# Modulation units of the front by feature tile, with the q and k products between them, and the decay product on four column tiles

## The chip, the core and the metric

One core of a Trainium2 chip runs the whole program. The metric is the device time of one launch in microseconds, the median of several executions. Everything is float32; an instruction of the matrix engine that is a product stands in the trace as two MATMULs.

## The reference

Two layers of a hybrid decoder step on 256 prompt tokens and 8 single decode tokens (264 columns in all), with 1024 features. What the change touches is the very start of layer 0:

```
m = silu(c) @ w_ada + b_ada                 # 9 conditioning rows -> 3 x 1024
shift, scale, gate = split(m, 3)
h = x * (1 + scale) + shift
z = h @ w_in                                # 1024 -> q 256, k 256, v 512, g 512, a_lr 16, u 1024
log_a = log_sigmoid(a_lr @ w_a2 + b_a) / 16 # 16 -> 256, the decay of the linear attention
glu = ua * sigmoid(ug)                      # u = [ua, ug]
```

After it come a gated linear attention over 4 heads, a causal convolution of 31 taps over 512 channels of `glu`, an output projection, layer norm, a mixture of 16 experts (each 3 matrices of 2 MB), and a second layer with a pooling mixer and another mixture.

## The kernel before

Features lie on the partitions: x and h are 8 tiles of 128 features by 264 tokens (`x[:, k, :]`, `h[:, k, :]`). Weights come in units of 2 MB, 128 partitions x 8 row tiles x 512 columns, into nine slots (six in `ring`). `load_plan` lists the units with their slots in the order in which SyncE issues them (L492 to L496, `fill`): the four modulation units of layer 0's shift and scale, `ada` 0 to 3 (each 512 columns of `w_ada`, in rows of 2 KB), then the unit of q and k (`qk`), the masks of `con` (L494), `ug`, `ua`, `v`, `g`. SyncE waits for a slot to be free (`unit_free`); the matrix engine waits for a unit by the slot's semaphore (`unit_ready`, with the count in `FILL`). ScalarE's queue loads x_prompt, x_sample and ten small vector tensors (L1092 to L1098). GpSimd's queue loads the 16 columns of the decay's first matrix (`walr`, L1854) and its second (`wa2`, L1856), then waits until all of h is there (`h0_ready` 8) and loads the convolution history, conv_w, the attention state (L1860 to L1866) and the router's matrices of both layers (ten loads of 16 KB, L1868 and L1871). The state lands where x_prompt was.

The order of work on the matrix engine is written out by hand. It transposes silu(c) (L811), runs modulation unit 0 (`ada_unit`: 32 instructions on four column tiles that give 9 rows, L567; ScalarE copies them, `ada_columns` at L586 turns them into columns), transposes the vectors (L817) and x (L825; ScalarE copies each tile, scaled), and runs units 1 to 3. Since unit i holds columns 512i to 512i + 511, units 0 and 1 are all the shifts and 2 and 3 all the scales: no tile of h can be made before unit 3 is through. VectorE then adds the bias (`ada_copy`), makes the samples' part of h in two operations and the eight tiles in eight (`modulate0`, L1403 to L1411), each tile a count of `h0_ready`.

`z_tile` (L831) makes the tiles of the projection in the order of `Z_TILES`: the decay's first product `alr` (L841: 8 products of 16 columns, each on a tile of h), q tile 0 (L850, 8 products), `la` 0 and 1 (L844, the decay's second product, which waits for the copy of `alr`), the other three of q and k, then level 0 of the attention (L868), then for each further level s two more tiles and the level: `ug0` and `ua0` before level 1, and so on. Bank numbers are in `Z_BANK`. VectorE and ScalarE make from `la` the log decay and its two running sums (L1487), on which level 1 rests, while level 0 needs only q and k.

Of the kernel before, what the change touches and what calls it, by code (L numbers as in the profile page):

```python
# [25 lines left out]
P = 128  # L26
# [3 lines left out]
NS = 8  # L30
# [73 lines left out]
FILL = {n: [s for m, s in PLAN[:i + 1] if len(m) == 2].count(SLOT[n]) for i, (n, _) in enumerate(PLAN)}  # L104
# [67 lines left out]
def build(nc, I, O):  # L172
    with ExitStack() as ctx:
# [75 lines left out]
        walr = t2f[:, 1536 + SEQ:1536 + SEQ + KD * 16].rearrange("p (k n) -> p k n", k=KD)  # L249
# [134 lines left out]

        def ada_slice(i):
            s, n = divmod(i, ADA_UNITS)
            return ksplit(I["w_ada"][s // 2, s % 2][:, FF * n:FF * (n + 1)])
# [27 lines left out]
        N_ROWS, N_SMALL, N_ROUTE, N_HIST = len(VEC_ROWS), 2, 14, 2  # L415
# [11 lines left out]
        Z_BANK = [0, 1, 2, 3, 4, 5, 0] + [4 + i % 2 for i in range(16)]  # L427
# [27 lines left out]
        def _(sp):  # L455
# [95 lines left out]
        def _(pe):  # L551
# [22 lines left out]
            def ada_columns():  # L574
# [4 lines left out]
                s, n = divmod(i, ADA_UNITS)  # L579
                taken = [p[:2] for p in PIECES].index((s, n)) if (s, n) in [p[:2] for p in PIECES] else 0  # L580
# [3 lines left out]
                for b in range(2):  # L584
                    o = ada_bank(i)[:, 36 * n:36 * (n + 1)].rearrange("p (h b w) -> p b h w", h=2, b=2)[:, b]
                    last = mm(o, ada_rows[:, i % 2, P * b:P * (b + 1)], fold, start=True, stop=True)  # L586
# [226 lines left out]
            ada_unit(0)  # L813
            pe.wait_ge(s_rows, 16 * N_ROWS)
            for i, n in enumerate((96, 90, 124)):
                o = (0, 96, 186)[i]
                last = tr(bank[4][:, o:o + n], rowsA[0:n, i, :], ident[0:n, 0:n])  # L817
            last.then_inc(E("opening_tr"), 1)
# [8 lines left out]
            for i in range(1, ADA_FRONT):  # L827
                ada_unit(i)
            ada_columns()

            def z_tile(i):  # L831
# [1148 lines left out]
```

## Time and profile before

| | us |
|---|---|
| median of 3 runs (lowest, highest) | 852.32 (851.91, 852.33) |
| profiled execution, in all | 850.87 |
| its span, from the first to the last instruction | 849.0 |
| matrix engine busy | 741.4 (87%) |
| VectorE, ScalarE, GpSimd busy | 240.7, 282.3, 130.0 |
| DMA, mean rate | 330 GB/s |
| mean granted clock of the matrix engine | 0.947 |

The stretch of the change is the first 60 to 70 us. Read the chain for what ends last, the timeline for durations, and the DMA views for what the queues move: q1 is SyncE's queue, q10 ScalarE's, q0 GpSimd's.

### The profile page before, as it was taken

Reading aid. Unit: us, or ns where it says so; the run is one execution under the profiler, and the core shown is the slowest. Engines: PE = TensorE matmul, PEld = TensorE weight load, DVE = VectorE, ACT = ScalarE, POOL = GpSimd, SP = SyncE. Lnnn points to the kernel's source line nnn. Section 1 sums busy time; section 2 is a strip of 40 time slices with the busy share of each in tenths; the row PEclk is TensorE's granted clock in tenths of the full one; section 3 lists DMA queues with packets and bytes.
Section 4 is the critical chain, followed back from the end, with each engine's and each line's share of the span. In section 5 each row is a group of like instructions: output and inputs, shape, how many; then the busy total and the mean of one; then the engine's idle time right before and its main releaser. Section 6 shows DMA issues by size and latency. Waiting matters only on the chain.

```text
span 849.0 us, 22536 instructions
## 1 busy us (share of the span) xinstructions
PE 741.4 (87%) x9606; PEld 463.7 (55%) x9607; DVE 240.7 (28%) x596; ACT 282.3 (33%) x571; POOL 130.0 (15%) x217
## 2 busy tenths in 40 slices
PE   3799999899999999897886789978999979889964
PEld 2378887575655555453443368644555535545532
DVE  1139998714700000000000381272000000000033
ACT  2135677412433333322131250142333223323323
POOL 0170687400001001000000000001101101000101
PEclk9899999799999999999897889999999989999985
DMA  9999523995994989999999999697899999999301
GB/s 313 390 239 359 199 100 119 339 340 201 410 381 192 370 329 405 420 425 426 419 421 417 382 368 407 231 396 308 339 426 415 428 417 426 420 423 424 139 0 51
DMA packets 63885, 280.48 MB, mean 330 GB/s; under 512 B 3013, under 2 KB 3627, under 8 KB 55638
## 3 DMA queue, kind: packets, MB, share of 16 engines
q1 hardware_dynamic: 60738, 271.75, 81.2%
q0 software_dynamic: 2432, 6.94, 2.6%
q10 hardware_dynamic: 676, 1.24, 0.5%
q8 instruction: 28, 0.46, 0.2%
q14 instruction: 11, 0.09, 0.0%
HBM read 277.49 MB, written 3.37 MB: 331 GB/s over the span
## 4 chain that ended last, share of the span: by engine, by line
PE 62%; DMA 21%; DVE 7%; ACT 4%; SPq 2%; issue 2%; POOL 0%; DVEq 0%; ACTq 0%
PE bank L716 17%; DMA ring<-in_w_up 13%; PE bank L850 9%; PE bank L726 7%; PE bank L988 7%; PE bank L689 5%; PE bank L751 4%; DMA big<-in_w_up 4%; DMA ring<-in_w_ada 3%; PE bank L567 3%; DVE t L1353 2%; PE bank L697 2%; ACT big L1291 2%; DMA big<-in_state_pool 2%; SPq L474 1%
## 5 line engine op out<-in xcount | busy, mean ns | idle before, releaser
L716 PE MATMUL bank<-ring,big 128*32 128x256 f32 x2112 | 128.9, 399 | 25.8 <-DMA ring<-in_w_up 22.5
L716 PEld LDWEIGHTS bank<-ring,big 128*32 128x32 f32 x2112 | 70.8, 115 | 79.7 <-DMA ring<-in_w_up 21.1
L1918 POOL TENSOR_TENSOR big<-t 128x192 f32<-128x192 f32 x51 | 26.4, 518 | 547.9 <-PE bank L689 411.7
L1787 DVE SCALAR_TENSOR_TENSOR big<-big,bank 128x128 f32<-128x128 f32 x49 | 17.0, 347 | 307.8 <-ACT big L1289 307.8
L689 PE MATMUL bank<-htm,big 128*32 128x256 f32 x1224 | 75.5, 379 | 1.2 <-POOL big L1921 1.2
L850 PE MATMUL bank<-big,ring 128*128 128x264 f32 x320 | 73.9, 389 | 0.0
L716 PE MATMUL bank<-big 128*32 128x256 f32 x1024 | 63.0, 401 | 9.8 <-DMA big<-in_w_up 6.5
L850 PEld LDWEIGHTS bank<-big,ring 128*128 128x128 f32 x320 | 60.0, 190 | 11.5 <-issue 0.8
L726 PE MATMUL bank<-ring,big 128*32 128x256 f32 x1056 | 63.8, 382 | 0.0
L1289 ACT ACT_TABLE_LOAD x49 | 62.9, 1283 | 1.7 <-issue 0.8
L567 PE MATMUL bank<-ring,cT 128*32 128x256 f32 x768 | 53.6, 426 | 10.2 <-DMA ring<-in_w_ada 9.7
L1298 ACT ACTIVATE big<-bank 128x256 f32<-128x256 f32 x49 | 18.8, 383 | 126.8 <-PE bank L726 126.8
L1289 ACT ACTIVATE big<-bank 128x128 f32<-128x128 f32 x49 | 13.6, 277 | 139.2 <-PE bank L716 139.2
L988 PE MATMUL bank<-big,ring 128*128 128x264 f32 x256 | 58.7, 389 | 0.0
L751 PE MATMUL bank<-big 32*128 32x256 f32 x816 | 58.4, 400 | 0.0
L1790 DVE TENSOR_SCALAR big<-con,big 128x288 f32<-128x288 f32 x49 | 18.1, 370 | 135.7 <-PE bank L751 135.7
L716 PEld LDWEIGHTS bank<-big 128*32 128x32 f32 x1024 | 34.7, 116 | 36.5 <-issue 10.3
L1891 POOL TENSOR_TENSOR t<-t,big 128x256 f32<-128x256 f32 x60 | 47.2, 786 | 41.8 <-ACT big L1157 33.4
L988 PEld LDWEIGHTS bank<-big,ring 128*128 128x128 f32 x256 | 48.1, 190 | 9.0 <-issue 1.2
L689 PEld LDWEIGHTS bank<-htm,big 128*32 128x32 f32 x1224 | 36.1, 110 | 19.5 <-POOL big L1921 1.7
L726 PEld LDWEIGHTS bank<-ring,big 128*32 128x32 f32 x1056 | 30.9, 109 | 27.9 <-issue 10.9
L567 PEld LDWEIGHTS bank<-ring,cT 128*32 128x32 f32 x768 | 25.5, 121 | 31.9 <-issue 21.0
(252 smaller groups left out, 842.2 us busy)
## 6 DMA issues: line engine op xcount, KB each, us to landing
ring<-in_w_ada SPq DMA_DIRECT2D x24, 2048.0 KB, 18.4
ring<-in_w_gate SPq DMA_DIRECT2D x21, 2048.0 KB, 22.6
ring<-in_w_up SPq DMA_DIRECT2D x21, 2048.0 KB, 24.8
ring<-in_w_down SPq DMA_DIRECT2D x21, 2048.0 KB, 26.5
big<-in_w_gate SPq DMA_DIRECT2D x11, 2048.0 KB, 15.3
big<-in_w_up SPq DMA_DIRECT2D x11, 2048.0 KB, 18.8
big<-in_w_down SPq DMA_DIRECT2D x11, 2048.0 KB, 19.0
ring<-in_w_in_even SPq DMA_DIRECT2D x5, 2048.0 KB, 33.1
```

The costliest lines, as they stand in the source:

```text
L567: last = mm(ada_rows_bank(i)[r:r + 32, 0:2 * P], cT[:, 9 * k:9 * k + 32], w[:, k, 2 * P * hf:2 * P * (hf + 1)], start=(k < 2), stop=(k >= ...
L689: last = mm(GATH[C * q:C * (q + 1), :], pk[:, t, :], htm[:, t, 2 * P * q:2 * P * (q + 1)], start=(t == 0), stop=(t == TT - 1), tile_positi ...
L716: last = mm(GU[C * q:C * (q + 1), :].rearrange("p (a n) -> p a n", a=2), hgc[:, P * (k % 2) + C * (k // 2):P * (k % 2) + C * (k // 2 + 1)] ...
L726: last = mm(Y[C * dq:C * (dq + 1), :], hidt[:, C * q:C * (q + 1)], wd[:, q, 2 * P * dq:2 * P * (dq + 1)], start=(q == 0), stop=(q == 3), t ...
L751: last = mm(SUM[2 * dq + b], ysb[r, P * b:P * (b + 1)], sct[r, 0:SEQ], start=False, stop=final and b == 1, tile_position=(C * dq, 0))
L850: last = mm(o[:, 0:T], w[:, k, P * n:P * (n + 1)], h[:, k, :], start=(k == 0), stop=(k == KD - 1))
L988: last = mm(bank[b0 + m % 4][:, 0:T], w[:, k, P * (m % 4):P * (m % 4 + 1)], src[:, k, :], start=(i == 0), stop=(i == KD - 1))
L1289: fn(silu, GU[:, 0:P], ACT.Silu).then_inc(m["silu_done"], 1)
L1298: fn(ysb, Y, ACT.Copy).then_inc(m["y_copied"], 1)
L1790: v.tensor_scalar(sct, tokens, tabs[:, bass.ds(g, 1)], None, ALU.is_equal)\
L1891: v.tensor_tensor(o, o, tapped[n % TAPPED], ALU.add)\
L1918: v.tensor_tensor(flat, all_r, all_b[:, :, bass.ds(g, 1)].broadcast_to([P, 2 * TT, C]), ALU.mult)\
```

## The change

The columns of `w_ada` are fetched in another grouping: front unit i now holds shift and scale of feature tiles 2i and 2i + 1 (256 columns of each, in two loads of 1 KB rows). `load_plan` puts the q,k unit second, between `ada` 0 and `ada` 1. The matrix engine transposes x before unit 0 and the vectors after it; `ada_columns` waits in the front for the tiles of h of the unit before (the `h0_ready` wait in the diff); after the columns of unit i VectorE makes tiles 2i and 2i + 1 of h (`modulate0(i)`), and the matrix engine adds their two row tiles to all four q and k tiles, which are kept open in four banks (`qk_parts`), before or after the next unit. The last two row tiles are added in `z_tile`. The decay's first product puts feature tile k on column tile k % 4, with `walr` widened with zeros to 32 columns, and its second sums over all 128 partitions, `wa2` lying four times at partitions 0, 32, 64 and 96, zero between. x_sample is loaded ahead of the sigmoid on ScalarE. Bank numbers of two tiles change.

```diff
 def load_plan():
-    plan = [(("ada", i), i) for i in range(4)]
-    plan += [(("in", n), s) for n, s in (("qk", 4), ("ug", 5), ("ua", 0), ("v", 1), ("g", 2))]
+    plan = [(("ada", 0), 0), (("in", "qk"), 4)] + [(("ada", i), i) for i in range(1, 4)]
+    plan += [(("in", n), s) for n, s in (("ug", 5), ("ua", 0), ("v", 1), ("g", 2))]
...
+        def front_source(i, half):
+            c = D * half + 2 * P * i
+            return ksplit(I["w_ada"][0, 0][:, c:c + 2 * P])
...
-        Z_BANK = [0, 1, 2, 3, 4, 5, 0] + [4 + i % 2 for i in range(16)]
+        Z_BANK = [0, 1, 0, 3, 4, 5, 2] + [4 + i % 2 for i in range(16)]
...
             def fill(name):
+                if name in FRONT:
+                    for i in range(2):
+                        sp.dma_start(slot(name, KD)[:, :, 2 * P * i:2 * P * (i + 1)], front_source(name[1], i))\
+                            .then_inc(unit_in[SLOT[name]], 16)
+                    return
...
 +                if 1 <= i < ADA_FRONT:
+                    pe.wait_ge(E("h0_ready"), 2 * i)
...
 -            for i in range(1, ADA_FRONT):
-                ada_unit(i)
             ada_columns()
+            def qk_part(j, n):
+                w = slot(("in", "qk"), KD)
+                for k in (2 * j, 2 * j + 1):
+                    last = mm(bank[Z_BANK[Z_TILES.index(("qk", n))]][:, 0:T], w[:, k, P * n:P * (n + 1)], h[:, k, :],
+                              start=(k == 0), stop=(k == KD - 1))
+                return last
+            def qk_parts(j):
+                pe.wait_ge(E("h0_ready"), 2 * j + 2)
+                for n in range(4):
+                    qk_part(j, n)
+            pe.wait_ge(E("x_copied"), KD)
+            unit_ready(pe, ("in", "qk"))
+            qk_parts(0)
+            ada_unit(1)
+            ada_columns()
+            qk_parts(1)
+            ada_unit(2)
+            ada_columns()
+            ada_unit(3)
+            ada_columns()
+            qk_parts(2)
...
                 if name == "alr":
                     pe.wait_ge(s_small, 16 * N_SMALL)
+                    pe.wait_ge(E("h0_ready"), KD)
                     for k in range(KD):
-                        pe.wait_ge(E("h0_ready"), k + 1)
-                        last = mm(o[0:16, 0:T], walr[:, k, :], h[:, k, :], start=(k == 0), stop=(k == KD - 1))
+                        q = k % 4
+                        last = mm(o[C * q:C * (q + 1), 0:T], walr[:, k, :], h[:, k, :], start=(k < 4), stop=(k >= 4),
+                                  tile_position=(0, C * q))
                 elif name == "la":
                     z_free(pe, 0)
-                    last = mm(o[:, 0:T], wa2[0:16, P * n:P * (n + 1)], alr[0:16, :], start=True, stop=True)
+                    last = mm(o[:, 0:T], wa2[:, P * n:P * (n + 1)], alr[:, :], start=True, stop=True)
+                elif name == "qk":
+                    last = qk_part(3, n)
...
-            def modulate0():
-                S.sync()
-                tt(h[:, :, SEQ:T], x[:, :, SEQ:T], ada[:, 0, KD:2 * KD, 1:9], ALU.mult)
-                S.sync()
-                tt(h[:, :, SEQ:T], h[:, :, SEQ:T], ada[:, 0, 0:KD, 1:9], ALU.add)
-                for k in range(KD):
+            def modulate0(i):
+                dve.wait_ge(E("ada_tr"), i + 1)
+                S.sync()
+                c = slice(2 * i, 2 * i + 2)
+                by_tile = lambda ap: ap[:, :, c]
+                tt(by_tile(ada[:, 0, 0:2 * KD, :].rearrange("p (h m) w -> p h m w", h=2)), front_columns(i),
+                   by_tile(vec[:, 0:2 * KD].rearrange("p (h m) -> p h m", h=2)).unsqueeze(3).broadcast_to([P, 2, 2, 9]),
+                   ALU.add, E("ada_copied") if i == ADA_FRONT - 1 else None)
+                S.sync()
+                scale = ada[:, 0, KD + 2 * i:KD + 2 * i + 2, :]
+                ts(scale, scale, 1.0, 1.0 / ALPHA, ALU.add, ALU.mult)
+                dve.wait_ge(E("x_copied"), 2 * i + 2)
+                S.sync()
+                tt(h[:, c, SEQ:T], x[:, c, SEQ:T], scale[:, :, 1:9], ALU.mult)
+                S.sync()
+                tt(h[:, c, SEQ:T], h[:, c, SEQ:T], ada[:, 0, c, 1:9], ALU.add)
+                for k in range(2 * i, 2 * i + 2):
                     ts(h[:, k, 0:SEQ], x[:, k, 0:SEQ], ada[:, 0, KD + k, 0:1], ada[:, 0, k, 0:1], ALU.mult, ALU.add,
                        E("h0_ready"))
...
-            pool.dma_start(walr, w_in[:, zcols["alr"]:zcols["alr"] + 16].rearrange("(k p) n -> p k n", p=P))\
+            B(v.memset(walr, 0.0))
+            B(v.memset(wa2, 0.0))
+            B.sync()
+            pool.dma_start(walr[:, :, 0:16], w_in[:, zcols["alr"]:zcols["alr"] + 16].rearrange("(k p) n -> p k n", p=P))\
                 .then_inc(s_small, 16)
-            pool.dma_start(wa2[0:16, :], I["w_a2"][0]).then_inc(s_small, 16)
+            for q in range(4):
+                pool.dma_start(wa2[C * q:C * q + 16, :], I["w_a2"][0]).then_inc(s_small, 16)
             pool.wait_ge(E("h0_ready"), KD)
```

## Rows read from the trace of the kernel before

**Rows 1.** The page: the chain that ended last, by engine

```profile
PE 62%; DMA 21%; DVE 7%; ACT 4%; SPq 2%; issue 2%; POOL 0%; DVEq 0%; ACTq 0%
```

**Rows 2.** The chain in order of time, 9 to 68 us: start, us, what, count

```profile
9.71 22.03 DMA ring<-in_w_ada
31.88 3.24 PE bank L567 x32
35.12 1.14 PE bank L586 x8
37.88 5.41 PE bank L841 x16
...
47.05 1.08 PE bank L844 x4
48.13 10.89 PE bank L850 x48
59.61 1.26 PE bank L868 x16
60.88 7.32 PE bank L850 x32
```

**Rows 3.** The `ua` unit's load: duration of the issue in ns, start, landing

```profile
L462 SPq DMA_DIRECT2D ring<-in_w_in_even x1: 6909/6909/6909, 29.0 to 29.0; - x1
...
DMA to landing us min/median/max: 34.8/34.8/34.8
```

**Rows 4.** DMA by queue (packets, MB, share of 16 engines), 44 to 54 us

```profile
GB/s 410 410 361 229 238 279 238 262 287 303 254 246 229 287 213 352 221 311 270 279 238 270 254 246 360 311 352 303 336 270 344 352 270 328 328 336 328 311 287 328
...
q0 software_dynamic: 540, 1.70, 58.7%
q1 hardware_dynamic: 607, 1.24, 44.9%
```

**Rows 5.** DMA by queue, 54 to 62 us

```profile
q1 hardware_dynamic: 418, 0.83, 90.1%
```

**Rows 6.** Busy time in windows: engines, granted clock, DMA share, GB/s

```profile
62.00:64.00 2.00, 2.00 (x10) 1.71 (x9) 1.86 (x5) 0.29 (x1) 0.00 (x0) 1.00 1.09 272
```

**Rows 7.** Packets in two full stretches, 20 to 34 and 210 to 230 us

```profile
DMA packets 2670, 5.41 MB, mean 387 GB/s; under 512 B 34, under 2 KB 34, under 8 KB 2669
...
DMA packets 1646, 8.20 MB, mean 410 GB/s; under 512 B 64, under 2 KB 64, under 8 KB 1335
```

**Rows 8.** Timeline: start, us, engine, line, what, idle before it

```profile
14.43 3.43 PE L567 MATMUL bank<-ring,cT 128*32 128x256 f32 x32 [5.49 <-DMA ring<-in_w_ada]
...
18.54 4.19 PE L825 MATMUL bank<-con,htm 128*128 128x128 f32 x24
...
26.16 1.93 PE L567 MATMUL bank<-ring,cT 128*32 128x256 f32 x32 [1.02 <-DMA ring<-in_w_ada]
...
36.28 0.31 DVE L1347 TENSOR_TENSOR ada<-bank,vec 128x144 f32<-128x144 f32 x1 [16.77 <-PE bank L586]
...
37.33 2.67 DVE L1350 TENSOR_SCALAR big<-x,ada 128x256 f32<-128x256 f32 x8
...
40.29 1.07 POOL L1860 DMA_DIRECT2D big<-in_state_conv  x2 [37.42 <-DVE big L1350]
...
51.58 3.58 POOL L1871 DMA_DIRECT2D wr<-in_w_fine  x4
...
53.84 1.27 DVE L1487 TENSOR_TENSOR_SCAN big<-con,big 128x256 f32<-128x256 f32 x2
```

**Rows 9.** Timeline of the matrix engine after two waits for weights

```profile
684.99 6.08 PE L716 MATMUL bank<-ring,big 128*32 128x256 f32 x64 [5.66 <-DMA ring<-in_w_up]
...
744.66 5.27 PE L716 MATMUL bank<-big 128*32 128x256 f32 x64 [3.39 <-DMA big<-in_w_up]
```

**Rows 10.** The chain again, a usual gate and up product

```profile
696.37 3.45 PE bank L716 x64
```

**Rows 11.** Windows again, right after the first of those waits

```profile
685.00:690.00 5.00, 5.00 (x48) 2.36 (x52) 0.00 (x0) 0.00 (x0) 0.00 (x0) 0.51 1.07 435
```

More of the change, by code:

```diff
@@ L103 @@
 SET_FILLS = [[1, 1], [2 + EXPERTS // 3, 1 + EXPERTS // 3]]
-FILL = {n: [s for m, s in PLAN[:i + 1] if len(m) == 2].count(SLOT[n]) for i, (n, _) in enumerate(PLAN)}
+FRONT = [("ada", i) for i in range(ADA_FRONT)]
+FILL = {n: [s for m, s in PLAN[:i + 1] + [(m, m[1]) for m in FRONT] if len(m) == 2].count(SLOT[n]) for i, (n, _) in enumerate(PLAN)}
 ORDER = [n for n, _ in PLAN]
@@ L585, in ada_columns @@
                     o = ada_bank(i)[:, 36 * n:36 * (n + 1)].rearrange("p (h b w) -> p b h w", h=2, b=2)[:, b]
+                    if i < ADA_FRONT:
+                        o = front_columns(i)[:, :, b, :]
                     last = mm(o, ada_rows[:, i % 2, P * b:P * (b + 1)], fold, start=True, stop=True)
@@ L812, in _ @@
             last.then_inc(E("opening_tr"), 1)
[L813 to L818, printed above, removed]
             pe.wait_ge(s_x, 32)
@@ L826, in _ @@
                 last.then_inc(E("opening_tr"), 1)
-            for i in range(1, ADA_FRONT):
-                ada_unit(i)
-            ada_columns()
+            ada_unit(0)
+            pe.wait_ge(s_rows, 16 * N_ROWS)
+            for i, n in enumerate((96, 90, 124)):
+                o = (0, 96, 186)[i]
+                last = tr(bank[4][:, o:o + n], rowsA[0:n, i, :], ident[0:n, 0:n])
+            last.then_inc(E("opening_tr"), 1)
+            ada_columns()
+            def qk_part(j, n):
[19 more added lines that the diff above has]
+            qk_parts(2)
             def z_tile(i):
@@ L1092, in _ @@
             act.dma_start(htm[:, 0:2, :], I["x_prompt"][0].rearrange("(t p) d -> p t d", p=P)).then_inc(s_x, 16)
+            act.wait_ge(E("htm_zeroed"), 1)
+            act.dma_start(htm[0:NS, 2, :], I["x_sample"][:, 0, :]).then_inc(s_x, 16)
             act.wait_ge(s_c, 32)
             A(fn(cs[0:9, 1, :], cs[0:9, 0, :], ACT.Sigmoid), E("c_sig"))
-            act.wait_ge(E("htm_zeroed"), 1)
-            act.dma_start(htm[0:NS, 2, :], I["x_sample"][:, 0, :]).then_inc(s_x, 16)
             for _, r, c, src in VEC_ROWS:
                 act.dma_start(rowsA[r:r + src.shape[0], c, :], src).then_inc(s_rows, 16)
-            ada_unit(0)
             for k in range(KD):
-                act.wait_ge(E("opening_tr"), k + 3)
+                act.wait_ge(E("opening_tr"), k + 2)
                 copy(x[:, k, :], bank[k % 4][:, 0:T], E("x_copied"), scale=ALPHA)
-            for i in range(1, ADA_FRONT):
+            for i in range(ADA_FRONT):
                 ada_unit(i)
@@ L1112, in z_tile @@
                 if name == "alr":
-                    copy(alr[0:16, :], b[0:16, 0:T], E("z_copied_a"))
+                    copy(alr[:, :], b[:, 0:T], E("z_copied_a"))
                 elif name == "qk" and n < 2:
@@ L1371, in _ @@
             S(v.tensor_copy(cT[:, 0:9 * KD], bank[5][:, 0:9 * KD]), E("cT_ready"))
-            dve.wait_ge(E("opening_tr"), 2)
+            dve.wait_ge(E("opening_tr"), KD + 2)
             S(v.tensor_copy(vec[:, :], bank[4][:, 0:V_ALL]))
@@ L1467, in layer_norm @@
                        ln_scaled[:, 1, KD * idx + k:KD * idx + k + 1], ALU.mult, ALU.add)
-            ada_copy(0, 0)
-            dve.wait_ge(E("x_copied"), KD)
-            modulate0()
+            for i in range(ADA_FRONT):
+                modulate0(i)
             for n in range(2):
```

7 lines of the change are left out of this document (5 added, 2 removed).

## Prediction

> **What bounds the kernel now.** I read the chain of waits by engine first: the matrix engine holds 62% of it and DMA 21% [rows 1]. Then the chain in order of time over the part that the diff touches [rows 2]. There the reader sees three things. Until 31.74 us the chain is a transfer, the fourth modulation unit (it lands 22.03 us after 9.71). From then the matrix engine has no long gap: the fourth unit 3.24 us, its columns, the modulation on VectorE, the decay product L841 5.41 us, the three tiles of q and k that follow `la` in one block of 10.89 us, level 0 at 59.61. Then come two tiles of 3.66 us each (7.32 together), `ug0` from 60.88 and `ua0` from 64.54. From level 0 on it is the matrix engine that ends last in every step of this stage, so whatever moves the start of `ua0` moves the rest of the kernel by the same amount; later waits on weights hang on slots that earlier products free, and shift with them.
>
> The transfers come next. The `ua` unit is issued at 29.0 and lands 34.8 us later, at 63.8 [rows 3]. So `ua0` starts only 0.7 us after its weights are there. That is the place to look: the front can be made much faster and still stand before `ua`. Why does `ua` land so late? It is the 2.1 MB behind `ug` in SyncE's queue (q1). In 44 to 54 us the rate falls after the first slices from 410 to some 230 to 300 GB/s, and q1 moves only 1.24 MB, because GpSimd's queue (q0) takes 58.7% of the engines [rows 4]. In 54 to 62 q1 moves 0.83 MB, 0.104 MB per us [rows 5], while the 16 KB router loads, whose issue goes on until 55 [rows 8], are worked off. Only in 62 to 64 does the rate come back, 272 GB/s [rows 6]. Undisturbed, q1 runs at 387 GB/s [rows 7]. GpSimd issues its first of these at 40.29, just when the last tile of h is ready (37.33 + 2.67 = 40.00) [rows 8]; the rate falls at 44.2 to 44.5.
>
> **The change, part by part.** All times are from the profiled execution: span 849.0, 850.87 us in all, 1.45 below the median of 852.32; I apply the difference to the median.
>
> *Load order and row length.* The q,k unit goes ahead of units 1 to 3, and these four units are fetched as two halves each, in rows of 1 KB instead of 2 KB. What one packet costs is seen from two stretches with the engines full: 2670 packets of 2026 bytes in 14 us are 83.9 ns each per engine, 1646 of 4982 bytes in 20 us are 194.4 ns [rows 7]. A line through both has 37.4 ns per 1000 bytes and 8 ns per packet. 1024 more packets per unit on 16 engines are then 0.5 to 0.6 us, 2.4 us for four; with 0.1 for the three extra small GpSimd loads, SyncE's stream is 2.5 us behind from the last unit on. Bounds: 0, and 5 us if a packet cost twice that (all of the front and `ua` 2.4 later: 854.4). The trace has no stretch of 1 KB rows of this queue, so 2.4 stands as the value on the line.
> The Trainium skill, "DMA: Bandwidth & Descriptors", table at the head, says that transfers of 512 bytes and more go at line rate. By that rule the split is free, and the time is that of the second rival below; the two stretches speak against it.
>
> *When h is complete.* Unit 3 lands at 31.74 + 5.4 (the q,k unit ahead of it, 2.1 MB at 387 GB/s) + 2.4 = 39.6. Start 0.14 later, 1.93 us at full clock [rows 8] (3.24 at half), columns with the copy before them 1.14, to 42.8. Then VectorE: one wide chain and eight tiles took 36.28 to 40.00; now a chain of four small operations (0.8, like those before 37.33) and two tiles at 0.334 (2.67 / 8), so 1.5. That is 44.3. It is later if unit 2 is: `qk_parts(1)` now stands on the queue ahead of unit 2, and waits itself for the tiles of unit 1. Unit 1 is third in the stream, as unit 2 is now, which starts at 26.16 after a wait for its load [rows 8]; with two units of longer rows ahead of its end that is 27.4. 1.93, 1.14 and 1.5 later, at 31.9, h tiles 2 and 3 are there; `qk_parts(1)` takes 16 x 0.227 = 3.6 (10.89 / 48 each), unit 2 runs 35.6 to 37.5, and unit 3 at 39.75 waits for its load alone. But with short work and waits between, a unit can fall on the half clock, as unit 3 does now (3.24 against 1.93 [rows 2, 8]); with unit 1 at half clock, or `qk_parts(1)` partly, h is complete at 45 to 45.9. I take 45.0 and keep 44.3 to 45.9.
>
> *The products.* The last columns are done at 43.5 (45.0 - 1.5), `qk_parts(2)` to 47.1. The decay product is now 16 instructions on four column tiles; priced as those of a modulation unit, also on four tiles (1.93 / 32), 1.0 instead of 5.41. At the least this is 0.9, at the most 16 x 0.227 = 3.6. To 48.1. The last quarter of q,k tile 0 0.9, `la` 1.08, three more quarters 2.7: 52.8; 0.6 for copy and release (59.02 to 59.61 now), level 0 at 53.4. Before it was 59.61. **The front has gained 6.2 us.** Level 0 takes 1.26, `ug0` 3.66, to 58.3; `ug` is in at 47.5 (39.6, 2.5 for the masks, 5.4).
>
> *Where it goes.* `ua0` now waits for `ua`. GpSimd's loads still start when h is complete, so the disturbance starts 4.2 after 45.0, at 49.2 (before: 44.2, 4.2 after 40.0). From 44.2 to 63.8 q1 moved 1.24 - 0.08 (its first 0.2 us) + 0.83 + 1.8 x 0.27 = 2.47 MB until `ua` was in [rows 4 to 6]. In the new order the stream is 5.0 - 2.5 = 2.5 us further when the disturbance starts, 0.97 MB. 1.50 MB are left: 1.16 in the first 9.8 us, 0.34 at 0.104 MB per us 3.3 us. `ua` lands at 49.2 + 13.1 = 62.3, and `ua0` starts at 62.4, 4.1 us after `ug0` has ended.
> After such a wait the array restarts at half clock. Two waits for weights show it: after 5.66 us idle the 64 products of L716 take 6.08, after 3.39 idle 5.27 [rows 9], against 3.45 [rows 10]; the granted clock right after the first is 0.51, the 1.2 GHz level [rows 11]. So 2.6 and 1.8; for 4.1 idle I take 1.8. 62.4 + 1.8 = 64.2 against 64.54: **the sum is -0.3 us, 852.0.**
>
> *At nothing.* The transposes of x (4.19 us) move from between two units into the 5.49 us wait before unit 0 [rows 8]; if they run longer there, unit 0 slips, but its tiles of h are wanted only when q,k is in, at about 21 (26.0 - 5.4 + 0.6). The x_sample load goes ahead of the sigmoid on ScalarE, which waits for c anyway. Two memsets and three loads more on GpSimd are 30 us ahead of their use. Four more issues on SyncE stand in a queue that is throttled by transfers. The decay's VectorE and ScalarE chain ends its scans 7 us after `la`: at 57, under the wait for `ua`. The state load comes 5.0 us later, like all of GpSimd's, and the product that VectorE makes of it stands ahead of level 2's work there, with 8.6 us of the matrix engine's (two tiles and a level) between; if `ua` came at 58, this or the scans would be late next, by about a microsecond.
>
> **Rivals.**
> 1. *h complete later, less of `ua` in the disturbance.* One unit more at half clock. At 45.9 the disturbance starts at 50.1, 3.4 us or 1.31 MB further, 1.16 are left, `ua` is in at 59.9, `ug0` ends 59.2, no cold restart: 60.1 - 64.54 = -4.4, 847.9. For: unit 3's half clock today. Against: the array has more to do between units than before.
> 2. *1 KB rows are free.* Everything until h is 2.4 earlier, so is `ua`: 59.9, and the sum is -2.7, 849.6.
> 3. *GpSimd's loads cost the stream little when they come later*, so that the matrix engine alone sets it: `ua0` at 58.4, 6.1 less, 846.2. Against: [rows 4, 5] show q1 with a full queue and still at 0.104 MB per us.
> 4. *Slower: the wait for `ua` with its cold restart.* If h is complete at the earliest (44.3), the disturbance starts at 48.5 with the stream only 1.8 us further: 1.78 MB left, 15.8 us, `ua` in at 64.3, `ua0` at 64.4 at half clock, 2.6 lost after 6.8 us of idleness: +2.5, 854.8. It decides from h complete at 44.6 or earlier (then +1.6). It is the odd case: the quicker the front, the later `ua`, since the disturbance starts with the front's end.
>
> **From these to the numbers.** Forecast (`ua` in at 61 to 63.5) 0.34; rival 1 0.22; rival 2 0.12; rival 3 0.08; rival 4 0.24. About what a measurement tells from no change is 0.2%, 1.7 us. Faster 0.42, same 0.34, slower 0.24. The forecast's own range is 850.6 to 853.8. Rivals 1 and 4 and the unsure start of the disturbance carry the range: 846.8 to 855.2.
>
> **What would show it.** Right: unit 3 lands near 39.6; the last tile of h at 45; L841's successor takes 1 us; level 0 at 53 to 54; a gap of 2 to 6 us on the matrix engine before `ua0`, released by the transfer into the ring, and `ua0` on half clock; `ua` in at 61 to 64. Wrong: no such gap (rivals 1 or 3), unit 3 in at 37 (rival 2), or a gap at level 1 (VectorE's state product or the decay chain instead of `ua`).

## The result, and the profile after

| | before | after |
|---|---|---|
| median of six runs on one chip, us | 852.12 | 855.58 |
| lowest, highest | 849.52, 853.03 | 854.03, 855.96 |
| profiled execution, its span | 850.87, 849.0 | 854.03, 852.2 |
| mean granted clock | 0.947 | 0.941 |

The ratio, formed over the executions of both kernels, is 1.0035 with a 95% interval of 1.0021 to 1.0050: slower by 3.0 us (the two medians of the table lie 3.5 apart). Forecast was 852.0, and 855.2 was the upper end.

The chain of the changed kernel in order of time (start, us, what, count) stands against [rows 2].

```profile
16.64 3.64 PE bank L582 x32
23.49 5.49 PE bank L852 x16
...
42.23 1.91 PE bank L582 x32
45.28 3.65 PE bank L852 x16
...
54.63 1.28 ACT L1184
57.91 1.27 DVE big L1543 x2
59.26 2.24 PE bank L915 x16
61.50 9.07 PE bank L897 x32
70.57 1.19 PE bank L915 x16
```

L582 is a modulation unit, L852 a pair of feature tiles of q and k (or one quarter), L915 a level, L897 the tiles between levels. Unit 3 runs at 42.2 and q and k follow, but then the chain leaves the matrix engine: ScalarE's table load (L1184) and VectorE's scans (L1543), and only at 59.26 level 0. It was at 59.61 in [rows 2]: six microseconds gained have become 0.35. Level 0 then takes 2.24 instead of 1.26 and the two tiles behind it 9.07 instead of 7.32, and level 1 is 2.4 us later than before (70.5 against 68.1).

The timeline shows what held level 0 and what else went wrong (start, us, engine, line, what, idle before and its releaser).

```profile
46.13 0.73 DVE L1396 TENSOR_SCALAR big<-x,ada 128x256 f32<-128x256 f32 x2
47.15 1.08 POOL L1920 DMA_DIRECT2D big<-in_state_conv  x2 [42.54 <-DVE big L1396]
48.86 1.10 PE L885 MATMUL bank<-big 128*32 128x264 f32 x16
50.89 1.05 PE L889 MATMUL bank<-stat,big 128*128 128x264 f32 x4
51.78 2.83 PE L852 MATMUL bank<-big,ring 128*128 128x264 f32 x12
...
54.63 1.28 ACT L1184 ACT_TABLE_LOAD   x1
...
56.57 0.93 ACT L1130 ACTIVATE big<-bank 128x264 f32<-128x264 f32 x3
...
57.91 1.27 DVE L1543 TENSOR_TENSOR_SCAN big<-con,big 128x256 f32<-128x256 f32 x2
59.13 0.06 DVE L1547 MEMSET epsb<- 128x1 f32 x1
59.26 2.24 PE L915 MATMUL bank<-big 64*128 64x128 f32 x16 [4.65 <-DVE epsb L1547]
61.43 9.14 PE L897 MATMUL bank<-big,ring 128*128 128x264 f32 x32
62.10 4.01 DVE L1393 TENSOR_TENSOR t<-big 128x256 f32<-128x256 f32 x2
63.07 2.76 POOL L1939 TENSOR_TENSOR big<-big 120x512 f32<-120x512 f32 x2
69.69 0.69 DVE L1393 TENSOR_TENSOR big<-big,t 128x512 f32<-128x512 f32 x1
```

First, `la` ends at 51.9 and the last q and k quarter at 54.6, all tiles that level 0 reads. But its start signal is VectorE's memset L1547, which stands in program order behind the whole decay: two operations on `la`, Exp and Ln on ScalarE with a table load each, the scans. ScalarE also copies the last three q and k tiles (L1130 x3) only behind the Ln. So level 0 waits 4.65 us. With `la` done the chain to the end of the scans takes 7.2 us (51.94 to 59.18).

Second, the two VectorE products of L1393 at 62.10 take 4.01 us. The same two took 0.76 in the kernel before, where GpSimd's product of the convolution history was long over. Here are that pair and that product in its timeline:

```profile
56.32 2.50 POOL L1879 TENSOR_TENSOR big<-big 120x512 f32<-120x512 f32 x2
...
62.91 0.76 DVE L1347 TENSOR_TENSOR t<-big 128x256 f32<-128x256 f32 x2
...
67.25 0.68 DVE L1347 TENSOR_TENSOR big<-big,t 128x512 f32<-128x512 f32 x1
```

Now GpSimd's product starts at 63.07, 6.75 us later, since its queue is released by the last tile of h (46.86 instead of 40.00), and it falls on VectorE's. VectorE's products for level 2 start at 69.69 instead of 67.25.

Third, the clock. The windows of the changed kernel (window, length, busy time and count of PE, PEld, DVE, ACT and POOL, granted clock, DMA share, GB/s):

```profile
49.00:54.00 5.00, 5.00 (x34) 3.81 (x30) 2.34 (x4) 2.09 (x4) 5.00 (x8) 1.00 1.06 328
54.00:62.00 8.00, 3.35 (x20) 2.63 (x19) 4.42 (x9) 5.60 (x9) 8.00 (x11) 0.76 1.06 289
62.00:66.00 4.00, 4.00 (x13) 3.17 (x12) 3.96 (x3) 0.00 (x0) 3.73 (x4) 0.62 1.08 122
```

Full until the gap; 0.76 and 0.62 behind it, so part of the time at the lower level, 1.2 GHz.

And the transfers, by the lines that answer to [rows 3]: unit 3's second half is issued at 28.1 and lands 11.9 later, at 40.0; `ua`'s is issued at 34.5 and lands 22.7 later:

```profile
L477 SPq DMA_DIRECT2D ring<-in_w_in_even x1: 2898/2898/2898, 34.5 to 34.5; - x1
...
DMA to landing us min/median/max: 22.7/22.7/22.7
```

That is 57.2, over two microseconds before level 0 ran: `ua` is never waited for.

From there on the kernels run in parallel: +2.4 us at level 1, +3.3 at the output projection (168.8 against 165.5), +3.4 at the first gate and up product of the experts (237.9 against 234.5), +3.2 at the end of the span. That last product's start is the mark used below ("first expert product"): it sums up the front and the attention. One execution of each kernel was traced, and the same front varies between them: level 0 of the changed kernel stands at 59.26, but in a kernel with the same front and the same hold (the filled gap, below) at 58.46. So marks less than a microsecond apart say nothing, and a total is judged by the median and the ratio.

### The profile page after: what moved, and what is told of

The parts are those of the page before. It is cut to its first block, busy times and chain, and to the rows that moved or that the text cites. A ratio compares the mean times of both kernels' runs of the same rounds, so it can differ in the third digit from the quotient of the medians.

```text
span 852.2 us, 22568 instructions
## 1 busy us (share of the span) xinstructions
PE 745.2 (87%) x9606; PEld 469.0 (55%) x9607; DVE 246.4 (29%) x608; ACT 281.8 (33%) x571; POOL 132.1 (15%) x222
## 4 chain that ended last, share of the span: by engine, by line
PE 67%; DMA 20%; DVE 4%; ACT 4%; SPq 2%; issue 2%; POOL 0%; DVEq 0%; ACTq 0%
PE bank L735 16%; DMA ring<-in_w_up 13%; PE bank L745 7%; PE bank L897 7%; PE bank L1035 7%; PE bank L708 6%; PE bank L582 4%; PE bank L770 4%; DMA big<-in_w_up 4%; PE bank L852 2%; PE bank L716 2%; DMA ring<-in_w_ada 2%; SPq L489 2%; DMA big<-in_state_pool 2%; ACT big L1337 2%
## 5 line engine op out<-in xcount | busy, mean ns | idle before, releaser
L735 PE MATMUL bank<-ring,big 128*32 128x256 f32 x2112 | 127.7, 396 | 28.1 <-DMA ring<-in_w_up 24.6
L735 PE MATMUL bank<-big 128*32 128x256 f32 x1024 | 58.4, 380 | 9.7 <-DMA big<-in_w_up 6.6
L745 PE MATMUL bank<-ring,big 128*32 128x256 f32 x1056 | 63.8, 382 | 0.0
L1335 ACT ACT_TABLE_LOAD x49 | 62.9, 1283 | 1.7 <-issue 0.9
L897 PE MATMUL bank<-big,ring 128*128 128x264 f32 x256 | 60.9, 398 | 0.0
L1035 PE MATMUL bank<-big,ring 128*128 128x264 f32 x256 | 58.8, 389 | 0.0
L582 PE MATMUL bank<-ring,cT 128*32 128x256 f32 x768 | 54.5, 432 | 1.6 <-DMA ring<-in_w_ada 1.1
L897 PEld LDWEIGHTS bank<-big,ring 128*128 128x128 f32 x256 | 49.3, 195 | 9.3 <-issue 0.2
L1035 PEld LDWEIGHTS bank<-big,ring 128*128 128x128 f32 x256 | 48.2, 190 | 9.0 <-issue 1.2
L770 PEld LDWEIGHTS bank<-big 32*128 32x128 f32 x816 | 36.9, 184 | 9.5 <-issue 8.2
## 6 DMA issues: line engine op xcount, KB each, us to landing
ring<-in_w_in_even SPq DMA_DIRECT2D x5, 2048.0 KB, 22.7
```

The costliest lines, as they stand in the source:

```text
L582: last = mm(ada_rows_bank(i)[r:r + 32, 0:2 * P], cT[:, 9 * k:9 * k + 32], w[:, k, 2 * P * hf:2 * P * (hf + 1)], start=(k < 2), stop=(k >= ...
L735: last = mm(GU[C * q:C * (q + 1), :].rearrange("p (a n) -> p a n", a=2), hgc[:, P * (k % 2) + C * (k // 2):P * (k % 2) + C * (k // 2 + 1)] ...
L745: last = mm(Y[C * dq:C * (dq + 1), :], hidt[:, C * q:C * (q + 1)], wd[:, q, 2 * P * dq:2 * P * (dq + 1)], start=(q == 0), stop=(q == 3), t ...
L770: last = mm(SUM[2 * dq + b], ysb[r, P * b:P * (b + 1)], sct[r, 0:SEQ], start=False, stop=final and b == 1, tile_position=(C * dq, 0))
L897: last = mm(o[:, 0:T], w[:, k, P * n:P * (n + 1)], h[:, k, :], start=(k == 0), stop=(k == KD - 1))
L1035: last = mm(bank[b0 + m % 4][:, 0:T], w[:, k, P * (m % 4):P * (m % 4 + 1)], src[:, k, :], start=(i == 0), stop=(i == KD - 1))
```

## The experiments

Fifteen kernels ran in four groups; ratios are against the kernel before on the same chip.

### The hold of level 0, the idle gap, the wait for `ua`

**Level 0 waits for its own tiles.** Changed kernel, but:

```diff
-                pe.wait_ge(E("level_qk"), s + 1)
+                if s == 0:
+                    z_free(pe, 1); z_free(pe, 2); z_free(pe, 6)
+                else:
+                    pe.wait_ge(E("level_qk"), s + 1)
```

> The changed kernel, in which level 0 waits for the copies of its own tiles (q, k, and the bank of la 0) and no longer for VectorE's memset, which stands behind the decay's scans. Theory A (the decay chain on VectorE's and ScalarE's queues holds level 0, and the half clock after the gap costs the rest): level 0 starts at about 57.6 instead of 59.26, since ScalarE copies the last three tiles only behind Ln (they end at 57.50); the gap shrinks from 4.65 to about 3 us, some half clock stays, 1 to 2.5 us less: 853 to 854.5. Theory B (the transfers hold the stage): level 0 as before, 855.6.

Measured: 854.16, ratio 1.0016 (1.0000 to 1.0033). Level 0 starts at 56.76 after 3.03 us of waiting, now released by ScalarE's copy. In this execution the memset comes at 58.24, so it would have held level 0 for 1.6 us more (the other 0.9 of the 2.5 us against 59.26 is an earlier front); the copies behind Ln do the rest. VectorE's pair takes 4.03 us at 61.20, and although level 1 starts at 66.80, 1.3 us earlier than before the change, the matrix engine waits 1.88 us at 119.6 and takes 9.07 us instead of 7.39 for the next two tiles; the first expert product is at 238.9. The median is inside theory A's range, but the interval overlaps that of the changed kernel (1.0021 to 1.0050), and the traced execution, 855.67, is no faster than it. The hold is real; what removing it alone gives back is between nothing and half of the loss.

**The copies on VectorE too.** In addition VectorE copies q tile 1 and both k tiles while ScalarE makes Exp and Ln:

```diff
-Z_BY = ["d" if nm in ("la", "ua") else "a" for nm, _ in Z_TILES]
+Z_BY = ["d" if nm in ("la", "ua") or (nm == "qk" and n) else "a" for nm, n in Z_TILES]
...
             tt(la2, la2, la, ALU.max, E("decay_dve"))
+            for i in range(4, 7):
+                dve.wait_ge(E("z_done"), i + 1)
+                ...
```

> As e1, and VectorE copies q tile 1 and both k tiles in the time in which it waits for ScalarE's Exp and Ln. Theory A: level 0 at about 55.2, no gap of more than 1 us, full clock, level 1 at about 64.3 instead of 70.5: some 6 us less, 849.5. Theory B (transfers): ua is in at 57 as in the changed kernel and its product is due at 60, so nothing should wait; were the stream slower here, ua0 would start only when ua is in. Theory C (ScalarE's and VectorE's later work, level_exp and level_diff, is the next to be late): level 1 starts at 66 or later, 851 to 853.

Measured: 854.46, ratio 1.0025 (1.0009 to 1.0040). The timeline of its matrix engine:

```profile
57.05 7.39 PE L897 MATMUL bank<-big,ring 128*128 128x264 f32 x32
64.37 1.26 PE L920 MATMUL bank<-big,htm 64*128 64x128 f32 x16
69.25 5.96 PE L897 MATMUL bank<-big,ring 128*128 128x264 f32 x18 [3.62 <-ACT big L1170]
```

The front's gain arrives at level 1, 3.7 us earlier than before the change, at full clock (level 0 stands at 55.89). Then the matrix engine waits 3.62 us: VectorE's pair took 4.04 us at 62.79, and its level 2 products came at 70.41. The traced execution is a long one of its kernel (856.80), but the median missed the ranges of A and of C as well. Something else than the start of level 0 takes the gain.

**Fill the gap.** The hold stays; nine products whose results nobody reads keep the matrix engine busy in it:

```diff
+            for i in range(9):
+                mm(bank[6][:, 0:T], ident, h[:, i % KD, :], start=True, stop=True)
             level(0)
```

> The changed kernel with nine products more (4.1 us, into a bank that nobody reads) between the last q,k tile and level 0, in the gap of 4.65 us. Theory A, its second half (the clock falls in the gap, and level 0, ug0 and ua0 take 2.24 + 9.07 instead of 1.26 + 7.32): level 0 still at 59.3, level 1 at 67.9 instead of 70.5, 2.6 us less, 853.0. If the clock has no part in it: no change, 855.6.

Measured: 855.78, ratio 1.0041 (1.0025 to 1.0057), no gain at all. Its matrix engine:

```profile
58.46 1.26 PE L915 MATMUL bank<-big 64*128 64x128 f32 x16 [0.67 <-DVE epsb L1549]
...
66.97 1.26 PE L915 MATMUL bank<-big,htm 64*128 64x128 f32 x16
...
118.51 1.26 PE L915 MATMUL bank<-big,htm 64*128 64x128 f32 x16
121.66 9.04 PE L897 MATMUL bank<-big,ring 128*128 128x264 f32 x32 [1.89 <-ACT big L1173]
```

The half clock was caused by the gap: filled, levels 0 to 7 run at full clock and level 1 stands at 66.97, 3.5 us earlier than in the changed kernel (2.7 by the clock, 0.8 by an earlier front in this execution). But VectorE's pair still takes 4.12 us (at 61.30), and at 121.66 the matrix engine waits 1.89 us and pays 1.65 more at half clock: all is given back. My theory that the gap and its clock are the whole loss fell here.

**The decay edit alone**, on the kernel before (`walr` widened, L841's product on four column tiles, the second sum over 128 partitions):

> The kernel before with the decay on four column tiles as the only change. h is complete at 40.0 as before, the decay's first product ends at about 41.5 instead of 43.3, all behind it is 1.9 earlier, level 0 at 57.7. The prediction's gate (ua in at 63.8): ua0 starts at 63.9 instead of 64.54, 0.6 less, 851.6, with a gap of about 1 us before it. Without that gate: 1.9 less, 850.3.

Measured: 852.55, ratio 1.0003 (0.9989 to 1.0017). Its matrix engine:

```profile
58.51 1.26 PE L870 MATMUL bank<-big 64*128 64x128 f32 x16 [0.61 <-DVE epsb L1493]
59.70 3.83 PE L852 MATMUL bank<-big,ring 128*128 128x264 f32 x16
64.56 3.80 PE L852 MATMUL bank<-big,ring 128*128 128x264 f32 x16 [1.03 <-DMA ring<-in_w_in_even]
```

Here the gate of the prediction is real: `ug0` ends at 63.53 (59.70 + 3.83) and `ua0` waits until 64.56 for `ua`, as early as before the change (64.54). Level 0 is only 1.1 us earlier (57.7 was expected): each decay product still waits for its own tile of h, so all of them take 3.25 us here, until 41.9.

### Where GpSimd's product falls

**GpSimd's loads early.** Its loads of history, conv_w and state start when four tiles of h are there, the product when all are, the router's loads after `ua0`.

```diff
-            pool.wait_ge(E("h0_ready"), KD)
+            pool.wait_ge(E("h0_ready"), 4)
             ... # history, conv_w, state
+            pool.wait_ge(E("h0_ready"), KD)
+            pool.wait_ge(s_conv, 96)
+            ... # the product, moved here
+            pool.wait_ge(E("z_done"), 9)
             ... # the router's loads
```

> The changed kernel with GpSimd's list in another order: the loads of the convolution history, conv_w and the state start when tiles 0 to 3 of h are there (33.6), the history's product follows when h is complete (46.9, VectorE idle until 51.5), the router's loads wait until ua0 is made. Theory D (VectorE stands for 3.3 us in level_diff(2), 62.1 to 66.1, while GpSimd makes this product, and so is as late as the matrix engine): level_diff(2) takes 0.8, VectorE starts level 2's q and k products at about 66.4 instead of 69.7. But the gap and the half clock before level 1 stay, level 1 at 70.5: little or nothing less in all, 854.5 to 855.6. If the stall alone made the loss: 853. Theory B (transfers): ua would be in early and the whole 3 us faster.

> g1 with the nine filler products of e3. If the loss has two causes side by side, half clock on the matrix engine (2.6 us at level 1) and the stall of VectorE (3.3), each of which alone keeps it, this is the kernel that gives it back: level 1 at 67.9, no wait for VectorE at level 8 (the tile pair that starts at 121.66 in e3 starts at 120.2), 852.0 to 853.0, that is as the kernel before. If only one mattered, this is like e3 (855.8).

> g1 with level 0 waiting for its own tiles, the three copies on VectorE as in e2, and the decay's first product between two halves of qk_parts(2), la right after q tile 0. The decay's la ends at 50 instead of 51.9, level 0 starts at 55.5 without a gap, ug0 and ua0 run to 64 at full clock, level 1 starts at 64 instead of 70.5 (68.12 before); VectorE is at level 2's products at about 65. The stage is then bound by VectorE, some 2.5 to 3.5 us ahead of the kernel before: 849 to 850. If ua or the state were late: 851 to 853.

Measured: 859.81 (ratio 1.0073, 1.0048 to 1.0099); with the filler 858.67 (1.0067, 1.0044 to 1.0090); with own tiles, copies on VectorE and the decay earlier 854.48 (1.0021, 1.0001 to 1.0040). All three missed, for a reason that I had not weighed; the traced execution is the slowest of each (860.06, 862.99 and 859.33), and the third kernel's twelve spread from 849.59 to 859.33, three of them near the forecast; what sets these apart can't be told from one trace. The first one's matrix engine:

```profile
47.71 3.23 PE L582 MATMUL bank<-ring,cT 128*32 128x256 f32 x32 [6.03 <-DMA ring<-in_w_ada]
...
65.84 2.24 PE L915 MATMUL bank<-big 64*128 64x128 f32 x16 [4.40 <-DVE epsb L1547]
```

Unit 3, at 42.16 in the changed kernel, waits for its load until 47.71 (48.1 and 48.3 in the other two). The early loads run beside the modulation units' and take the rate from them: in 40 to 47.6 us SyncE's queue moved 1.07 MB and GpSimd's 1.00, together 273 GB/s. These runs say nothing of what the product costs, but they show what holding GpSimd's loads back until h is complete was good for.

**The collision in the kernel before.** One added wait holds GpSimd's product until the first level's Exp:

```diff
             pool.wait_ge(s_conv, 96)
+            pool.wait_ge(E("level_exp"), 1)
             for i in range(2):
                 ins = B(v.tensor_tensor(conv_prod[0:4 * HIST, i, :], ...
```

> The kernel before with GpSimd's product of the convolution history held until ScalarE's first Exp of the levels is done (61.5 instead of 56.3), so that it falls on VectorE's q and k products or on level_diff(2). Nothing else is changed. Theory D: one of VectorE's operations there takes 2 to 3.3 us more, level 2's products start at about 70 instead of 67.25, and since the matrix engine has only about half a microsecond of lead over VectorE at the last levels, the kernel is 2 to 3 us slower: 854 to 856. If the stall costs nothing (the matrix engine has more lead): 852 to 853.

Measured: 856.29, ratio 1.0045 (1.0028 to 1.0061). VectorE and the matrix engine of it:

```profile
62.10 1.75 DVE L1347 TENSOR_TENSOR htm<-big,t 128x512 f32<-128x512 f32 x1
63.88 1.71 DVE L1347 TENSOR_TENSOR t<-big 128x256 f32<-128x256 f32 x2
...
121.81 7.39 PE L850 MATMUL bank<-big,ring 128*128 128x264 f32 x32 [1.46 <-ACT big L1125]
```

Front and level 0 are as before; only the 2.50 us of GpSimd's product have moved to 61.54, where they take 3.44. VectorE is 1.9 us later at level 2 (69.17) and the matrix engine waits 1.46 from 120.35 on, so that level 8 is 1.4 us late (129.13 against 127.69). Then come more products at half clock than before in the stretch from 133 to 157 (a modulation unit takes 3.64 at 153.55, where it took 1.93), and the output projection starts at 168.66, 3.2 late. The first expert product is at 237.75. So this collision alone costs the kernel before about as much as the whole change did.

**The product left out**, of the changed kernel, without and with the filler:

> The changed kernel without GpSimd's product of the convolution history (two operations of 120 x 512 left out, so the samples' part of the convolution is not computed), loads and all waits as they are. Theory D (the product stalls VectorE's level_diff(2) for 3.3 us): level_diff(2) takes 0.8, level 2's products on VectorE start at 66.4 or, where the state's load (in at 63) is waited for, a little later, instead of 69.7. The half clock on level 0, ug0 and ua0 stays and level 1 is still at 70.5, so the matrix engine alone holds: 0 to 1 us less, 854.6 to 855.6.

> p1 (history product left out) with the nine filler products of e3 in the gap before level 0. If half clock and stall are two causes side by side, both are gone: level 1 at 67.9, no wait at level 8, 852.0 to 852.5, some 3 us below the changed kernel and as the kernel before. If the stall does not matter, as e3: 855.8.

Measured: 846.01 (0.9940) and 842.49 (0.9908). The totals can't be compared: the samples' changed values send tokens to other experts, and there are 3072 gate and up instructions instead of 3136, one chunk fewer. Up to the experts the marks are good: level 1 at 70.05 and the first expert product at 236.51 without the filler; 67.85 and 234.32 with it, as before the change (68.12 and 234.47). And VectorE's pair is as fast as before the change, though every load of GpSimd's queue stands where the changed kernel has it:

```profile
61.83 0.76 DVE L1393 TENSOR_TENSOR t<-big 128x256 f32<-128x256 f32 x2
```

So it is the product that slows the pair, and not the loads ahead of it.

### The two causes, each alone and together

The product moves into the time in which VectorE waits for Exp and Ln, and the loads start when unit 3 is in, so that they don't delay it:

```diff
-            pool.wait_ge(E("h0_ready"), KD)
+            pool.wait_ge(E("h0_ready"), 2)
+            pool.wait_ge(unit_in[3], 32)
             ... # history, conv_w, state
+            pool.wait_ge(E("decay_dve"), 1)
+            pool.wait_ge(s_conv, 96)
+            ... # the product
+            pool.wait_ge(E("z_done"), 9)
             ... # the router's loads
```

> The whole of the reference's work is done here. The changed kernel; GpSimd starts the loads of history and state when unit 3 is in, makes the history's product while VectorE waits for ScalarE's Exp and Ln (54 to 56.7), and loads the router's matrices after ua0. The matrix engine's part is as in the changed kernel. Two causes side by side: level_diff(2) takes 0.8 and VectorE is 3 us ahead, but level 0 at 59.3 with the half clock keeps level 1 at 70.5: the first gate and up product comes about 1.4 earlier than in the changed kernel (as with the product left out), 853.5 to 855. The stall alone: 852.

> r1 with the nine filler products in the gap before level 0. Both causes gone with all work done: level 1 at 67.9, the first gate and up product at 234.4 (234.47 in the kernel before, 237.87 in the changed one), 851.5 to 852.5, as the kernel before. If the loss is not these two: 854 or more.

| median, ratio, first expert product | gap before level 0 | gap filled |
|---|---|---|
| product on VectorE's level work | 855.58, 1.0035, 237.9 | 855.78, 1.0041, 239.2 |
| product in VectorE's wait | 855.10, 1.0035, 237.5 | 850.99, 0.9992, 233.4 |

The last ratio's interval is 0.9982 to 1.0003, that of the one to its left 1.0022 to 1.0048. In the medians, removing either cause gives nothing back; removing both gives 0.4%. (With the product left out altogether, the first expert product came 1.4 us earlier than in the changed kernel, with the filler too 3.6.) The matrix engine of the kernel with both removed:

```profile
58.39 1.26 PE L915 MATMUL bank<-big 64*128 64x128 f32 x16 [0.39 <-DVE epsb L1549]
59.58 7.39 PE L897 MATMUL bank<-big,ring 128*128 128x264 f32 x32
66.90 1.26 PE L915 MATMUL bank<-big,htm 64*128 64x128 f32 x16
```

This trace is the fastest of its eleven executions, with a front 0.7 us earlier than its neighbour's; the ratio rests on all of them. In the kernel without the filler, VectorE's pair is back at 0.76 (at 61.90) and its level 2 products at 66.25, but the gap of 4.39 us is there and the clock with it: level 0 takes 2.24, the two tiles 9.56, and level 1 starts at 70.72.

Why the two don't add: in the levels two engines run almost full side by side. The window of the kernel before over levels 0 to 8:

```profile
59.00:129.00 70.00, 69.40 (x399) 57.74 (x399) 65.19 (x99) 43.26 (x81) 34.19 (x43) 1.00 0.63 211
```

The third pair, VectorE, is at 65.19 of 70 us, the first, the matrix engine, at 69.40. In the changed kernel the gap leaves the matrix engine 2.4 us late at level 1, the collision leaves VectorE 2.4 us late at level 2's products; the later of the two sets the pace.

**The front without the decay edit** (changed kernel, decay one product after another on 16 columns):

> The changed kernel with the decay as before: 8 products of 16 columns one after the other, la over 16 partitions (the front by feature tile alone is left of the change). The first product of the decay then takes 3.6 instead of 1.1, la, Exp, Ln and scans are 2.5 later, and level 0, which stands behind them on VectorE, starts at 61.8 instead of 59.3, after a gap of 7 us: 2.5 to 4 us more than the changed kernel, 858 to 860. If level 0 were held by q and k alone: under 1 us more, 856.

Measured: 858.22, ratio 1.0073 (1.0058 to 1.0088). The decay product takes 3.73 us instead of 1.10, level 0 starts at 62.89 with the same wait (4.29 for VectorE), GpSimd's product meets VectorE again (4.01). Level 0 is 3.6 us later than with the edit. What was worth nothing in the kernel before is worth some 3 us here (0.0038 of the ratio): there `ua` came next, here the decay's chain does.

### A version that beats both

On top of the product in the wait, level 0 waits for its own tiles, and the decay product stands in the middle of the third pair of q and k, as soon as h is complete. The second kernel also runs unit 2 ahead of the second pair.

```diff
-            qk_parts(2)
+            pe.wait_ge(E("h0_ready"), 6)
+            qk_part(2, 0)
+            qk_part(2, 1)
...
-            for i in range(7):
+            for i in range(4):
+                z_tile(i)
+            qk_part(2, 2)
+            qk_part(2, 3)
+            for i in range(4, 7):
                 z_tile(i)
             level(0)
```

> Toward a kernel that beats both: the changed kernel in which GpSimd starts its loads of the history and the state when unit 3 is in (40.1, not in front of it as in g1, which delayed unit 3 by 8 us), makes the history's product while VectorE waits for ScalarE's Exp and Ln, and loads the router's matrices after ua0; level 0 waits for its own tiles; the decay's first product stands in the middle of qk_parts(2), la behind q tile 0. la is done at 50.2 instead of 51.9, the scans at 57.6, level 0 at 56.3, level 1 at 65, VectorE at level 2's products at 64.8 (69.7 in the changed kernel, 67.25 in the kernel before). If VectorE's chain holds the levels: 2.4 ahead of the kernel before, 849.7. If the state's load or ua comes late (in at 52 and 58 expected): 851 to 852.

> g7 with unit 2 and its columns ahead of qk_parts(1). Unit 2 (in at 34.0) then runs at 34.1 instead of 39.1, qk_parts(1) beside the wait for unit 3, unit 3 starts at 41 instead of 42.2: h complete at 45.6 instead of 46.9, everything behind it 1.2 earlier than g7: 848.5. If the matrix engine's half clock eats it: as g7.

Measured: **848.87, ratio 0.9971 (0.9958 to 0.9985)**, and 849.99, 0.9979 (0.9964 to 0.9995). The first one's matrix engine:

```profile
55.48 1.24 PE L922 MATMUL bank<-big 64*128 64x128 f32 x16 [1.00 <-ACT big L1141]
...
60.66 3.80 PE L899 MATMUL bank<-big,ring 128*128 128x264 f32 x16 [0.18 <-DMA ring<-in_w_in_even]
64.39 1.26 PE L922 MATMUL bank<-big,htm 64*128 64x128 f32 x16
```

Level 0 is 4.1 us earlier than in the kernel before, and now `ua0` waits 0.18 us for `ua`: the gate of the prediction is close. So is VectorE's and ScalarE's level work, for which the matrix engine waits 0.23 us at 116.70. The first expert product is 3.3 us earlier (231.16), but the first one of layer 1 only 0.6 (579.43 against 580.04). The traces show where the lead goes: it is 1.8 us at the products that start at 525.90 in layer 1 (527.68 before), so 1.5 are gone by then and 1.2 more by 579. Why was not tested, and the two traced executions (850.56 and 850.87) are closer than the kernels' ratio says. Unit 2 earlier brought no more, and it did not bring what it was made for: unit 2 ran at 34.25, but took 3.45 us instead of 1.94, unit 3 stood at 42.45 and h was complete at 47.15, against 42.03 and 46.73. Level 1 is at 64.39 in both.

## Why the prediction was wrong

**The failed step** is "level 0 at 53.4", and under it the sentence of the text ahead that "level 0 needs only q and k". By its data it does, by its start signal it doesn't: the signal comes from VectorE's queue, behind the decay's chain, and the last copies stand on ScalarE's queue behind Ln. The trace of before showed it: the scans begin at 53.84 [rows 8], late in a block of q and k products that starts at 48.13 and runs until 59.0 [rows 2]. The chain ran under that block, hidden; the change moved the block's work ahead of `la` and took the cover away. Of the 5.9 us by which level 0 missed 53.4, 1.9 are h's, complete at 46.9 instead of 45.0, and 4.0 the signal's. I looked at this chain and set it against the wait for `ua`, "under" which it would end at 57; it ended at 59.1, and nothing was left to hide it. The consequences follow by themselves: of "the front has gained 6.2 us" 0.35 was left, `ua` was there in time, so that the gap before `ua0`, the centre of the forecast, never came; it stood one step earlier, before level 0, and brought the half clock with it. That restart cost 2.7 us after 4.65 us of idleness (2.24 and 9.07 instead of 1.26 and 7.32), more than the 1.8 taken for 4.1.

**The cause not in the list at all** is GpSimd's product. I moved its loads in the sum ("all of GpSimd's" come later), followed the state to VectorE and stopped there; the product behind the loads in the same queue I did not cost. It stood in the page as an operation beside an idle VectorE; 6.75 us later VectorE is nearly full.

**A smaller miss:** h complete at 45.0 became 46.9. The first two pairs of q and k ran at a granted clock of 0.68, that is in part at half clock (5.49 and 5.52 against 3.6), and unit 2, whose weights were in at 34.0, stood behind the second until 39.11; so unit 3 ran at 42.16 instead of 39.75. What this was worth at the end stays open: the kernel with unit 2 first was made to show it, but its h was complete no earlier.

**What held.** Unit 3's weights at 39.6: 40.0. The price of 1 KB rows: the halves of units 1 to 3 land at 24.95, 27.96, 30.97, 33.95, 37.03 and 40.01, so 6.0 us per unit, 0.6 more than the 5.4 of 2 KB rows, as forecast; rival 2 is out, and the rule of the Trainium skill ("DMA: Bandwidth & Descriptors", table at the head) that 512 bytes and more go at line rate does not fit: the units in 1 KB rows took 11% longer than those in 2 KB rows. The decay product 1.0: 1.10. The columns, levels and tiles: as sized. That `ua` comes later when h is complete earlier: 57.2 with h at 46.9, against 63.8 with h at 40.0; worked out by the prediction's own rates, h at 46.9 gives an estimate of 57.7. The gate by `ua`: seen in the decay edit alone and met in the best version. Rival 4 forecast 854.8 and a half-clock restart after a gap, but by the wait for `ua`; its time was near, its mechanism wrong, and that was luck. Rival 1's condition came true, h late and `ua` in time, and yet its 847.9 is 7.7 us off: it too let level 0 start when its data were there. Rival 3 (`ua` no limit, 846.2) has the same fault. The front's own work was right: the last q and k product ends at 54.6, which is 52.8 and h's 1.9. Where it waits was not.

**What stays open.** Of the 3.3 us at the output projection, 2.4 are there at level 1 and are explained; the 0.9 that join between 130 and 158, where a modulation unit runs at half clock (3.62 at 152.79, against 1.93 before), were not tested. The kernel in which GpSimd's product was held shows the same slow unit behind a delay of 1.4 us only. And the kernel with unit 2 first has it too (3.64 at 148.94): level 1 at 64.39 as in its neighbour, level 8 0.7 us later, the output projection 3.3 (165.29 against 162.01). With one trace of each, whether this belongs to the kernel or to the execution is not shown.

## What to carry to other kernels

When work is moved ahead of a signal's cover, follow the signal, not the data: list what stands before it on the queue of the engine that sends it, and how long that chain is once nothing runs beside it. Where two engines run nearly full side by side, look at both after every shift; a fix of one of them alone can measure as nothing. And move a queue with everything in it: an operation that cost nothing beside an idle engine has a price beside a busy one.

## What the runs showed of the hardware

- **GpSimd against VectorE.** When GpSimd multiplies two 120x512 float32 tiles, VectorE's two-input products nearly stop: 4.01 us instead of 0.76 for a pair (4.03, 4.04, 4.12 and 4.01 in four more kernels), or 1.75 and 1.71 for 0.68 and 0.76 when GpSimd's took 3.44 instead of 2.50. In the changed kernel the pair begins at 62.10 and would be over by 62.9, before the 63.07 that the trace gives as the product's start; by these starts alone one would not have seen the collision, which the kernel without the product shows. The Trainium skill ("GPSIMD Engine Reference", 8. Key points) says that the two share their SBUF interfaces and contend on instructions with two SBUF inputs; the traces agree and give the price.
- **Loads of GpSimd's queue beside 1 KB rows.** In the first kernel with early loads 1.44 MB of them, moved in 33 to 48 us (3.7 us at the 387 GB/s of [rows 7]), delayed unit 3 by 5.5 us on the matrix engine, and its landing from 40.0 to 47.6. That is more than their bytes explain: the two queues together moved 273 GB/s in 40 to 47.6, where SyncE's alone had moved 7.12 MB in 20 to 40 us of the changed kernel (356 GB/s). Whether GpSimd's longer packets are the reason was not tested.
- **Short gaps.** After 1.89 us idle at 119.8 the next two tiles took 9.04 us instead of 7.39; after 1.46 idle they took 7.39.
- **Half clock without a gap** (lines as in the windows above). In 133 to 137 us of the kernel before, the matrix engine is busy for 4.00 of 4.00 us at a granted clock of 0.57, and in 148 to 156 of the changed one for 8.00 of 8.00 at 0.65:

```profile
133.00:137.00 4.00, 4.00 (x16) 3.11 (x13) 3.90 (x10) 3.32 (x8) 3.43 (x5) 0.57 0.52 194
```
```profile
148.00:156.00 8.00, 8.00 (x99) 6.09 (x96) 7.46 (x9) 2.40 (x8) 7.20 (x10) 0.65 0.75 262
```
